# Modulation and first projection weights laid out by the host, 16 KB in one piece per partition and unit

## The reference

```python
# first block
mod = jax.nn.silu(c) @ w_ada[l] + b_ada[l]              # w_ada: 1024 x 6144
sh1, sc1, g1, sh2, sc2, g2 = jnp.split(mod[:, None, :], 6, axis=-1)
h = layer_norm(x) * (1 + sc1) + sh1
proj = h @ w_in[l]                                       # w_in: 1024 x 7680
uv, qkv, gates = jnp.split(proj, [UV_COLS, UV_COLS + QKV_COLS], axis=-1)
# second block
mod = jax.nn.silu(c) @ w_mod[l] + b_mod[l]               # w_mod: 1024 x 6144
mod_c = jax.nn.silu(c_ctx) @ w_mod[l] + b_mod[l]
```

## Time and profile before

| | us |
|---|---|
| median of 3 runs | 4577.94 |
| lowest and highest | 4568.46, 4580.52 |
| the profiled execution's own time | 4577.97 |
| its span, first to last instruction | 4576.1 |
| modulation stage in it | 0 to 196.5 |
| first_mix in it | 196.5 to about 640 |

### The profile page before, as it was taken

One profiled execution on the slowest core, in us unless ns is written; L12 is line 12 of the kernel. 1 busy time (PEld: TensorE's weight loads), 2 busy tenths in 40 slices (PEclk: granted clock), 3 DMA queues, 4 the chain that ended last, 5 costly groups with the idle time before them and its releaser, 6 DMA issues. The chain is left out here.

```text
span 4576.1 us, 37326 instructions
## 1 busy us (share of the span) xinstructions
PE 3691.0 (81%) x12048; PEld 1690.5 (37%) x12049; DVE 1840.0 (40%) x4015; ACT 610.2 (13%) x1457; POOL 828.0 (18%) x880
## 2 busy tenths in 40 slices
PE   7689999749889988998829847997677787787777
PEld 3234554323233322333315535763333333333333
DVE  1611222422222222222240254422366776776775
ACT  0011222000000000000000201110122222222221
POOL 0000000021001100101000040000244444444443
PEclk9799999859999999999959866578899999999999
DMA  9761122057998896587741000021499999999997
GB/s 330 226 111 58 65 67 89 35 188 300 390 370 334 350 410 252 229 341 296 317 177 55 6 0 1 1 83 46 160 427 427 427 427 427 427 427 425 423 419 311
DMA packets 211600, 1127.20 MB, mean 246 GB/s; under 512 B 23959, under 2 KB 25415, under 8 KB 95888
## 3 DMA queue, kind: packets, MB, share of 16 engines
q0 software_dynamic: 87712, 579.89, 31.5%
q1 hardware_dynamic: 123776, 545.91, 30.7%
HBM read 1100.35 MB, written 25.50 MB: 246 GB/s over the span
## 5 line engine op out<-in xcount | busy, mean ns | idle before, releaser
L2152 PE MATMUL ps<-q_uv,q_dg 128*128 128x512 f32 x2048 | 1004.4, 648 | 301.9 <-ACT q_dg L2178 301.7
L1136 PE MATMUL ps<-e_wt,e_xT 128*64 128x512 f32 x3200 | 747.8, 625 | 109.4 <-DMA e_wt<-in_w_exp 108.6
L2263 DVE SCALAR_TENSOR_TENSOR mod<-q_uv,mix 128x1024 f32<-128x1024 f32 x512 | 627.8, 1226 | 372.4 <-DMA q_uv<-in_peer_uv,q_picks 371.9
L2136 POOL DMA_INDIRECT q_uv<-in_peer_uv,q_picks x512 | 591.7, 1156 | 845.7 <-PE ps L2152 642.7
L2152 PEld LDWEIGHTS ps<-q_uv,q_dg 128*128 128x128 f32 x2048 | 414.8, 208 | 890.9 <-issue 890.9
L1136 PEld LDWEIGHTS ps<-e_wt,e_xT 128*64 128x64 f32 x3200 | 244.6, 144 | 602.9 <-issue 454.1
L1136 PE MATMUL ps<-e_wt,e_aT 128*64 128x512 f32 x1600 | 357.1, 599 | 21.8 <-ACT e_aT L1189 21.8
L498 PE MATMUL ps<-hT,ring 128*128 128x512 f32 x640 | 283.6, 601 | 14.4 <-ACT qkv L617 12.9
L1095 POOL DMA_INDIRECT scratch_y<-e_yb,e_row x50 | 49.7, 994 | 975.3 <-DVE e_yb L1251 975.3
L1136 PEld LDWEIGHTS ps<-e_wt,e_aT 128*64 128x64 f32 x1600 | 115.2, 138 | 231.6 <-issue 231.6
L1189 ACT COPY e_aT<-ps 128x512 f32<-128x512 f32 x50 | 29.3, 585 | 1176.6 <-PE ps L1127 1176.6
(11 more groups left out here) (422 smaller groups left out, 3457.4 us busy)
## 6 DMA issues: line engine op xcount, KB each, us to landing
e_wt<-in_w_exp SPq DMA_DIRECT2D x384, 1024.0 KB, 10.5
ring<-in_w_in SPq DMA_DIRECT2D x15, 2048.0 KB, 8.0
mod_ring<-in_w_ada SPq DMA_DIRECT2D x12, 2048.0 KB, 9.6
mod_ring<-in_w_mod SPq DMA_DIRECT2D x12, 2048.0 KB, 7.8
p_ring<-in_w_in SPq DMA_DIRECT2D x5, 2048.0 KB, 8.0
c_y<-scratch_y SPq DMA_DIRECT2D x4, 2048.0 KB, 14.4
r_ring<-in_peer_wq SPq DMA_DIRECT2D x4, 2048.0 KB, 9.0
q_uv<-in_peer_uv,q_picks POOLq DMA_INDIRECT x512, 20.6
```

What stands on the lines that cost most here:

```text
L1136: ins = nc.tensor.matmul(ps[64 * h:64 * h + 64, at, :], lhs[:, k % 4, 64 * (k // 4):64 * (k // 4) + 64], wt[:, u, a, h * W:(h + 1) * W], s ...
L2136: pool.indirect_dma_start(out=uv[:, n % NR, :, :].rearrange("p a d -> p (a d)"), out_offset=None, in_=A["peer_uv"], in_offset=bass.Indirec ...
L2152: last = nc.tensor.matmul(acc(t)[:, c, :], dg[:, n % ND, :], uv[:, n % NR, 1, c * W:(c + 1) * W], start=first, stop=last_one)
L2263: dve.scalar_tensor_tensor(junk[:, n % 2, :], uv[:, n % NR, 0, :], 1.0, h3[:, k // PH, :], ALU.mult, ALU.mult, accum_out=ap[:, k % 2, j:j ...
```

## The change

The host lays the three matrices out anew before the launch. `w_ada`, `w_mod_2` and `w_in` become arrays of units: for unit j and partition p, the eight pieces of 512 floats that this partition needs stand one after the other, 16 KB in one piece. The buffers in SBUF, the matmuls that read them, the number and order of all DMA instructions, and every semaphore are as before. In the instruction lists the source and destination shape of these loads goes from 128x8x512 to 128x4096. `w_branch_a`, which uses the same ring, keeps its layout. The gate units are number 11 to 14 of `w_in`.

```diff
--- before.py
+++ after.py
@@ -146,8 +146,7 @@
                 for n, (w, j) in enumerate(units):
                     if n >= NB:
                         sp.wait_ge(s_full, last_of[n - NB] + 1)
-                    sp.dma_start(ring[:, n % NB], A[w].rearrange("(k p) n -> p k n", p=P)[:, :, j * W:(j + 1) * W]
-                                 ).then_inc(s_landed[n % NB], 16)
+                    sp.dma_start(ring[:, n % NB].rearrange("p k n -> p (k n)"), A[w + "_units"][j]).then_inc(s_landed[n % NB], 16)
 
             @block.gpsimd
             def _(pool):
@@ -385,8 +384,8 @@
                         if name[:2] == "wa":
                             src = A["w_branch_a"].rearrange("(k p) n -> p k n", p=P)[:, :, int(name[2]) * W:(int(name[2]) + 1) * W]
                         else:
-                            c0 = G0 + (2 * (name[1] == "b") + int(name[2])) * W if name[0] == "g" else n * W
-                            src = A["w_in"].rearrange("(k p) n -> p k n", p=P)[:, :, c0:c0 + W]
+                            j = 11 + 2 * (name[1] == "b") + int(name[2]) if name[0] == "g" else n
+                            src = A["w_in_units"][j].rearrange("p (k w) -> p k w", k=KD)
                         sp.dma_start(ring[:, n % NB, 0:src.shape[1]], src).then_inc(s_landed[n % NB], 16)
                         while tiles and last_output[tiles[0]] <= 4 * (n - NB) + 8:
                             leave(tiles.pop(0))
@@ -2400,6 +2399,9 @@
     inputs["w_exp"] = np.concatenate([gate, up, down], 1).transpose(0, 1, 3, 2, 4).reshape(NE, NUNIT, P, 2 * D)
     rows = np.stack([np.asarray(inputs.pop(n)).reshape(NE, 2, W) for n in ("b_gate", "b_up", "b_down")], 2)
     inputs["b_exp"] = np.repeat(rows, 2, axis=1).reshape(NE, 4, 3 * W)
+    for n in ("w_ada", "w_mod_2", "w_in"):
+        w = np.asarray(inputs.pop(n))
+        inputs[n + "_units"] = w.reshape(KD, P, -1, W).transpose(2, 1, 0, 3).reshape(-1, P, KD * W)
     for name, a in inputs.items():
         a = np.ascontiguousarray(a)
         if a.shape[0] == 1:
```

## The result

| | before | after |
|---|---|---|
| median of 20 runs, us | 4576.94 | 4586.34 |
| lowest and highest | 4568.43, 4584.56 | 4578.77, 4589.45 |
| ratio to before, 95% interval | | 1.0019 (1.0012 to 1.0026) |
| profiled execution, own time (span) | 4577.97 (4576.1) | 4582.93 (4581.1) |

The medians lie 9.4 us apart; the ratio makes the cost 8.7 us (5.5 to 11.9). A second measurement of the same kernel gave 4583.0 against 4576.36 us, 6.6 us apart; its ratio of 1.0013 (1.0004 to 1.0022) makes 6.0 us. The two profiled executions of the table differ by 5.0 us only. The forecast was 4585.9 us.

A forecast was written before the change was run, and what follows sets the result against it. PE is busy 81% and most weight loads are covered; PE or DVE waits for transfers at four places. Terms -0.5 - 1.0 + 4.6 + 3.3 + 1.5 = +7.9 us on 4577.97 give 4585.9 us, range 4567 to 4595.

The forecast's parts named there:

- Term 1: Modulation start: unit 0, which PE's first matmul waits for, lands sooner at the higher rate; -0.5 us.
- Term 2: Modulation: DVE's 3.76 us wait for unit 22, at 172.24 us, gets shorter; -1.0 us.
- Term 3: Start of first_mix: const_buckets, on GpSimd's queue behind six rel_bias loads, lands later beside 16 KB weight packets; +4.6 us.
- Term 4: Before PE's stall in first_mix: scratch_lines stores take longer, alternating with unit 4's large packets; +3.3 us.
- Term 5: Same first_mix stall: from gm_ln_b's issue to DVE's start takes longer beside unit 5's large packets; +1.5 us.
- Rival A: GpSimd's queue q0 is not held up by weight packets, so only the rate counts; 4576.5 us, chance 0.25.
- Rival B: Before PE's first_mix stall, today's 2 KB packets slow the stores, so large ones shorten them; 4567.8 us, chance 0.13.
- Rival C: In first_mix nothing overlaps with a weight packet: stores, gm_ln_b and buckets all come later; 4597.2 us, chance 0.13.
- Rival D: The pieces are not 16 KB on the chip, transfers still being cut by 512 columns; 4578 us, chance 0.04.

The follow-up runs named there:

- e3: The changed kernel, but units 0 to 2 of w_in are loaded in 2 KB packets; ratio to before 1.0007.
- e4: The changed kernel, but w_in is loaded in 2 KB packets from unit 3 on; ratio to before 1.0003.
- e5: The changed kernel, but each unit, still one contiguous block of memory, is read in 2 KB packets; ratio to before 1.0003.
- e7: The changed kernel, but SP issues its first w_in unit only when the rel_bias loads and const_buckets have landed; 4575.12 us, ratio to before 1.0000.
- e2: The changed kernel, but modulation units are loaded in 2 KB packets as before, only w_in in 16 KB; 4586.72 us, ratio to before 1.0026.
- e10: e9, but w_in is loaded in 2 KB packets again, modulation in 16 KB; 4574.89 us, ratio to before 0.9996.
- e8: The changed kernel, but SP issues gm_ln_g and gm_ln_b after unit 2, instead of GpSimd behind the scratch_lines stores; 4562.95 us, ratio to before 0.9974.
- e9: The changed kernel with the changes of e7 and e8 together; 4556.36 us, ratio to before 0.9950.
- e6: The changed kernel, but w_in units are loaded in 8 KB packets, modulation in 16 KB; ratio to before 1.0004.

## Why the prediction was right, point by point

- **Term 1, unit 0, -0.5.** PE starts at 25.09 us against 25.21 in the first pair. Over all traces: 25.2 to 25.6 us in the four with 2 KB modulation packets, 24.6 to 25.1 in those with 16 KB, about 0.5 less. The rate from 20 to 24 us is 422 GB/s in after and 414 to 446 in the ten traces with 16 KB, 386 to 388 in the four with 2 KB. Right.
- **Term 2, unit 22, -1.0.** DVE's wait is 2.89 us against 3.76; 2.8 to 2.9 in every kernel with 16 KB, 3.8 to 4.2 in every one with 2 KB. Right. Terms 1 and 2 together: first_mix starts at 195.1 us on the mean of ten traces with 16 KB and at 196.8 on that of the four with 2 KB, -1.7 against -1.5.
- **Term 3, const_buckets, +4.6.** +4.8 in the first pair, +5.1 between the means. Right, with its mechanism: it follows units 0 to 2 alone (e3, e4), the packet's size and not the place in memory (e5), and is gone without company (e7). In 200 to 206 us, of after, the two queues take exactly equal turns:

```profile
q1 hardware_dynamic: 148, 2.16, 90.5%
q0 software_dynamic: 148, 0.00, 1.8%
```

  The turns have the length that was counted: in after the first packet of q0 starts 4.2 us after the first `rel_bias` issue (4.8 was counted), and the 192nd, after 12 turns on each engine, 7.7 us later, 0.64 us for a turn. The working was wrong in one detail that cancels: it took the 5.1 us from issue to landing for the load's own time and said that q0 never queues up beside 2 KB packets. Alone the load takes 1.9 us, and the weights cost 4.5 us of L already before the change (e7).

- **Term 4, the stores, +3.3.** +2.9 in the first pair; S is 94.8 to 97.5 us (mean 96.1) in five traces with small later units and 98.3 to 98.8 (mean 98.5) in four with large ones and an unchanged program, so +2.5. Slightly too large. The detail was wrong: unit 3 was to be through in 10 us. It is issued at 266.3 us and has landed by 293 us (26.0 and 26.8 us after the issue in e2 and e3), where before it took 48.4 us. The queues from 266 to 293 us, of after:

```profile
q0 software_dynamic: 815, 1.26, 46.0%
q1 hardware_dynamic: 144, 2.10, 19.5%
```

  Eight packets per engine in up to 27 us are about 3 us for each and not 1.2. And 815 to 144 packets are no equal turns: over this stretch q0 gets several packets, many of them tiny, for one of weights. In e10 the turns beside the stores are equal (47 to 46). Why they are not here was not tried. In e7, e8 and e9, with large packets too, S is 100.9 to 103.2 us; each of them issues other transfers beside the stores or has the stores earlier, and what this costs them was not tried either.
- **Term 5, gm_ln_b, +1.5.** Not found. G is 9.0 us on the mean of five traces with small later units (7.1 to 10.1) and 9.0 on that of four with large ones (8.0 to 9.9). The step that failed is the count of eight full turns of unit 5 against `gm_ln_b`. That small shifts decide which of the two goes first is likely but not shown: unit 5 is issued 0.2 us after `gm_ln_b` in after and 2.1 us before it in the second trace of after (G 7.96 and 9.06), and G is shortest, 7.13 us, in e4, where unit 5 follows 4.3 us later. With term 5 gone and term 4 smaller the stall did not grow to 17.7 us either; it was 12.57 and 15.96 us, against 12.90 and 13.65 before.
- **The sum, +7.9.** The parts as measured are -1.7 + 5.1 + 2.5 + 0 = +5.9. PE's restart after the stall shows it too: 329.75 and 327.13 us before, 333.75 and 334.55 after, 5.7 us between the means. The first load of the next stage, first_merge, is issued at 787.5 and 785.4 us before and at 792.0 and 792.7 after, 5.9 us between the means, so the places found account for what was lost in the stages that were changed. The medians differ by 9.4 and 6.6 us, the ratios make 8.7 (5.5 to 11.9) and 6.0 (1.8 to 10.1), and both intervals hold 5.9. That 4585.9 met 4586.34 so closely is partly luck, then: term 5 was 1.5 too high, term 4 by 0.8, and of the first 9.4 us some 3.5 lie beyond the places found. The spans of the two pairs of traces differ by 7.4 us between the means, 1.5 more than at the start of first_merge, and the experts stage, which scatters by 3 us whatever the packets, holds as much (1323.1 against 1321.6 us). Where the rest of the 3.5 is, and whether it is more than scatter, stays open.
- **Rival A** (q0 not held up) falls with L. The Trainium skill, page DMA: Bandwidth & Descriptors, section Queues, rings and completion order, lets a turn hold 9 to 17 descriptors; 148 against 148 packets in the rows above, of 16 KB on the one side, speak against it here. The 47 to 46 of e10 do so too. **Rival B** (the 2 KB packets slow the stores) has the wrong sign. **Rival C** (nothing overlaps) asked for S = 105 and L = 17.3; the means are 98.5 and 16.0. **Rival D** falls with the packets.

## What to carry to other kernels

Larger packets raise the rate of a load by about a tenth here (386 to 388 against 414 to 446 GB/s), and that is worth something only where an engine waits for that load. On a DMA engine shared by two queues they also shift the balance by turns: the small transfers of the other queue wait longer (+5 us here), while the queue with large packets gets through beside slow stores with an eighth of the packets (18.5 us between e9 and e10). So look for who waits for a transfer on the other queue before changing a packet's size, keep the bulk loads away from it by a wait, and take small loads out from behind long stores. With both done the large packets pay, 4556.4 us against 4574.9 with small ones; before takes 4576.4. A kernel with 2 KB packets and the second repair alone was not run. It would not start its units late, as e10 does, so how much of the 20 us needs the new layout is open.

## What was not expected of the hardware

- Equal turns hold for packets from 4 bytes to 24 KB: 67 to 67 and 191 to 190 before, 148 to 148 after, and 47 to 46 in e10, where one side is a store. They do not hold in 266 to 293 us of after, 815 to 144, beside the same stores.
- PE's wait for the six small `rel_bias` loads and the buckets ends 6.3 us after their first issue when nothing runs beside them, 10.9 beside 2 KB packets, 12.5 beside 8 KB (one trace) and 16.0 beside 16 KB. Beside weights the first small packet starts 4.0 to 4.3 us after the issue, alone 1.3 us (before, e6, after and e7).
- An issue can hold SP for long: that of a load of 256 KB took 44.10 us in e10, where the first of the two such loads takes 0.33 us in e9. The second of the two takes 14.69 us in e9 and 14.24 in e8, where SP's queue moved only 20 packets in the 18 us around it. What the issue waits for was not tried.
